# Norm factors and a bias row sent through memory, and gate sums scanned on VectorE, in place of fp32 products on TensorE

## What is computed

```python
def swiglu_ffn(x, g, w_gate, w_up, w_down):
    h = rms_norm_2(x, g)                       # x * rsqrt(mean(x*x) + eps) * g, a factor per token
    return (silu(h @ w_gate) * (h @ w_up)) @ w_down

# second block, forgetting attention: 8 heads, log_f is (256 tokens, 8 heads)
log_f = log_sigmoid(ff + b_forget)
cum = cumsum(log_f, axis=1).transpose(0, 2, 1)             # per head, along the tokens
logits = logits + cum[:, :, start:end, None] - cum[:, :, None, :end]

# second block, sparse attention: a bias per head and per bucket of the distance t - s (32 buckets)
bias = rel_bias[bucket]
```

## Time and profile before

| | us |
|---|---|
| median of three runs | 1117.91 (1117.83 to 1118.14) |
| the profiled execution, device time | 1117.82 |
| its span, first to last instruction of the program | 1116.0 |
| PE busy | 1110.3 (99%) |
| DVE busy | 786.0 (70%) |
| ACT busy | 621.3 (56%) |
| POOL busy | 57.7 (5%) |

### The profile page before, as it was taken

One profiled execution on the slowest core, in us unless ns is written; L12 is line 12 of the kernel. 1 busy time (PEld: TensorE's weight loads), 2 busy tenths in 40 slices (PEclk: granted clock), 3 DMA queues, 4 the chain that ended last, 5 costly groups with the idle time before them and its releaser, 6 DMA issues.

```text
span 1116.0 us, 14890 instructions
## 1 busy us (share of the span) xinstructions
PE 1110.3 (99%) x5854; PEld 944.4 (85%) x5854; DVE 786.0 (70%) x1112; ACT 621.3 (56%) x825; POOL 57.7 (5%) x105
## 2 busy tenths in 40 slices
PE   9999999999999999999999999999999999999998
PEld 8888888888888888888888888888888788888887
DVE  6777754766887677775477787557898686777752
ACT  6556542677566455564346556337787854656540
POOL 1000000100000000000000000021343000000000
PEclk9999999999999999999999999999999999999999
DMA  9765565644454656655565555557643455665550
GB/s 317 250 189 189 190 244 190 209 158 144 162 193 157 207 188 189 189 189 189 189 208 187 190 189 189 189 154 256 223 146 122 150 176 166 189 190 193 191 180 38
DMA packets 142581, 208.02 MB, mean 186 GB/s; under 512 B 9296, under 2 KB 100584, under 8 KB 142512
## 3 DMA queue, kind: packets, MB, share of 16 engines
q1 hardware_dynamic: 139408, 198.07, 54.1%
q0 software_dynamic: 3088, 9.00, 2.4%
q10 hardware_dynamic: 16, 0.00, 0.0%
HBM read 205.98 MB, written 2.65 MB: 187 GB/s over the span
## 4 chain that ended last, share of the span: by engine, by line
PE 96%; ACT 2%; DVE 1%; issue 1%; DMA 0%; SPq 0%; DVEq 0%
PE banks L1800 27%; PE banks L1686 16%; PE banks L1688 16%; PE banks L1687 16%; PE banks L1797 14%; PE banks L1758 1%; PE banks L2031 1%; PE banks L1708 1%; PE banks L1976 1%; ACT w_hi L751 0%; DMA raw<-in_ffn_w_gate 0%; PE banks L2061 0%; DVE w_lo L1138 0%; PE banks L2009 0%; PE banks L2058 0%
## 5 line engine op out<-in xcount | busy, mean ns | idle before, releaser
L1138 DVE TENSOR_TENSOR w_lo<-raw,w_hi 128x2048 fp32r<-128x2048 f32 x186 | 422.8, 2276 | 167.0 <-ACT w_hi L751 166.6
L751 ACT ACTIVATE w_hi<-raw 128x2048 fp32r<-128x2048 f32 x186 | 352.2, 1897 | 111.9 <-PE banks L1688 108.2
L1800 PE MATMUL banks<-xT,w_hi 128*128 128x512 f32 x1344 | 314.3, 390 | 0.0
L1800 PEld LDWEIGHTS banks<-xT,w_hi 128*128 128x128 f32 x1344 | 249.3, 188 | 49.8
L1797 PEld LDWEIGHTS banks<-xT,w_lo 128*128 128x128 f32 x1344 | 167.4, 191 | 4.1 <-DVE xg L1152 0.7
L1686 PE MATMUL banks<-w_hi,xT 128*128 128x512 f32 (+1 forms) x432 | 170.4, 394 | 0.0
L1797 PE MATMUL banks<-xT,w_lo 128*128 128x256 f32 x1344 | 169.8, 283 | 0.2
L1688 PE MATMUL banks<-w_hi,xT 128*128 128x512 f32 (+1 forms) x432 | 166.9, 386 | 0.0
L1687 PE MATMUL banks<-w_lo,xT 128*128 128x512 f32 (+1 forms) x432 | 166.7, 386 | 0.0
L1686 PE MATMUL banks<-w_hi,hT_hi 128*128 128x512 f32 x352 | 137.3, 390 | 0.0
L1688 PE MATMUL banks<-w_hi,hT_lo 128*128 128x512 f32 x352 | 137.0, 389 | 0.0
(11 more groups left out here) (315 smaller groups left out, 902.6 us busy)
## 6 DMA issues: line engine op xcount, KB each, us to landing
raw<-in_ffn_w_gate SPq DMA_DIRECT2D x88, 512.0 KB, 3.9
raw<-in_ffn_w_up SPq DMA_DIRECT2D x88, 512.0 KB, 4.9
raw<-in_ffn_w_down SPq DMA_DIRECT2D x88, 512.0 KB, 4.3
raw<-in_w_in SPq DMA_DIRECT2D x76, 512.0 KB, 4.5
raw<-in_w_out SPq DMA_DIRECT2D x16, 512.0 KB, 4.2
raw<-in_w_branch_moba SPq DMA_DIRECT2D x4, 512.0 KB, 4.2
raw<-in_w_branch_sb SPq DMA_DIRECT2D x4, 512.0 KB, 5.2
raw<-in_w_branch_a SPq DMA_DIRECT2D x4, 512.0 KB, 4.3
```

Source lines behind the costliest of these rows:

```text
L751: act.activation(w_hi[u % SLOTS][:, 0:n], raw[u % RAWS][:, 0:n], ACT.Copy).then_inc(hi_done, 1)
L1138: dve.tensor_tensor(w_lo[r][:, 0:n], raw[r][:, 0:n], w_hi[u % SLOTS][:, 0:n], ALU.subtract).then_inc(lo_done, 1)
L1800: m = pe.matmul(bank[b + s], mh, xT[:, k].rearrange("p a s -> p (a s)"), start=first, stop=k == KC - 1, skip_group_check=c == 0)
```

## The change

Three things are replaced, and the table of one-hot values is no longer sent to the chip.

Norm factors: in each of the four FFN phases POOL waits for the factors, writes them as a row to memory (`norm_rows`, 256 elements of 4 bytes), waits for that, and reads the row repeated on 128 partitions into `rstd_rows`, which now has a buffer of its own. DVE waits for this transfer ahead of its first `pair_scale`. The diagonal, the product and the copy are gone, and with them PE's waits for them.

Bias row: POOL reads the table transposed (8 by 32, elements of 4 bytes) and writes `lag_rows` by one copy for each range of distances that shares a bucket, 32 of them, in F0 right after the first gain transfer. The product, ACT's copy and the one-hot transfer are gone; the writing to memory and the spread there (L671, L673) follow right after, earlier than before.

Gate sums: the item CU is gone. POOL writes `log_f` transposed to memory by two transfers of 1024 elements of 4 bytes, waits for both, and reads it back as 8 rows of 256. In slot 14 DVE waits for that, sums along the rows by one scan, turns the sign and copies the first half. POOL's chain to the masks then starts from there.

```diff
-        out = [(6, "TR", ("iq", 0)), (7, "TR", ("iq", 1)), (9, "TR", ("ik", 0)), (12, "CU", ())]
+        out = [(6, "TR", ("iq", 0)), (7, "TR", ("iq", 1)), (9, "TR", ("ik", 0))]
...
+            rstd_rows = hid.enter_context(nc.sbuf_tensor("rstd_rows", [P, SEQ], F32))[:]
...
+        log_in = cum_last[0:NH, SC:SC + SEQ]
...
-        rstd_diag = gate[:, 0, 0:SEQ]
-        rstd_rows = gate[:, 1, DM:DM + SEQ]
-        onehot = gate[0:32, 1, 0:SC]
+        bias_cols = gate[0:NH, 1, 0:32]
...
+            def spread_rows(ph):
+                f, g = FFN_OF[ph], GAIN_OF[ph]
+                pool.wait_ge(rstd_done, g + 1)
+                pool.dma_start(norm_rows[f].rearrange("(t p) -> p t", p=P), rstd[:, 2 * g:2 * g + 2],
+                               allow_slow_non_contiguous=True).then_inc(rstd_out, 16)
+                pool.wait_ge(rstd_out, 16 * (f + 1))
+                pool.dma_start(rstd_rows, norm_rows[f].partition_broadcast(P)).then_inc(rows_in, 16)
...
-            pool.dma_start(onehot, a["onehot"]).then_inc(table_in, 16)
-            pool.dma_start(lgt[0:32, 0:NH], a["rel_bias_2"]).then_inc(table_in, 16)
+            pool.dma_start(bias_cols, a["rel_bias_2"].rearrange("b h -> h b"), allow_slow_non_contiguous=True)\
+                .then_inc(table_in, 16)
             pool.wait_ge(hi_done, 4)
             pool.dma_start(const[:, P:C_ONE], a["consts"][:, P:C_ONE]).then_inc(const_in, 16)
             pool.dma_start(tri_le, a["consts"][:, C_LE:C_GE]).then_inc(const_in, 16)
+            spread_rows("F0")
             for m in range(1, 7):
...
                 pool.dma_start(gain[m % 2][:], a[gains[m]].partition_broadcast(P)).then_inc(gain_in, 16)
+                if m == 4:
+                    spread_rows("F1")
+                    spread_rows("F2")
                 if m == 1:
+                    pool.wait_ge(table_in, 16)
+                    for k, (c0, c1) in lag_ranges():
+                        ins = pool.tensor_copy(lag_rows[:, c0:c1], bias_cols[:, k:k + 1].to_broadcast([NH, c1 - c0]))
+                    ins.then_inc(vrow_sb, 1)
                     pool.wait_ge(vrow_sb, 1)
...
-            cu = [it for it in ITEMS[1] if it.kind == "CU"][0]
-            pool.wait_ge(read_a, cu.read)
+            pool.wait_ge(rows_ready, 3)
+            for t in range(TT):
+                pool.dma_start(log_rows[:, t * P:(t + 1) * P].rearrange("h p -> p h"), lgf[:, NH * t:NH * t + NH],
+                               allow_slow_non_contiguous=True).then_inc(log_out, 16)
+            pool.wait_ge(log_out, 32)
+            pool.dma_start(log_in, log_rows).then_inc(log_row_in, 16)
+            pool.wait_ge(summed, 1)
             pool.dma_start(cum_rows, ncum).then_inc(cum_out, 16)
...
+            spread_rows("F3")
...
-                for tt in range(TT):
-                    dve.tensor_scalar(rstd_diag[:, tt * P:(tt + 1) * P], ident, rstd[:, 2 * g + tt:2 * g + tt + 1],
-                                      None, ALU.mult).then_inc(diag_done, 1)
...
-                    dve.wait_ge(rows_copied, FFN_OF[ph] + 1)
+                    dve.wait_ge(rows_in, 16 * (FFN_OF[ph] + 1))
...
+                def sum_log():
+                    dve.wait_ge(log_row_in, 16)
+                    link(dve.tensor_tensor_scan(ncum[:, P:SC], log_in, log_in, 0.0, ALU.add, ALU.min))
+                    link(dve.tensor_scalar(ncum[:, P:SC], ncum[:, P:SC], -1.0, None, ALU.mult))
+                    dve.tensor_copy(ncum[:, 0:P], ncum[:, P:SEQ]).then_inc(summed, 1)
...
+                        if slot == 14:
+                            sum_log()
...
-                if c == 2 and p == 1:
-                    pe.wait_ge(rows_copied, FFN_OF[ph] + 1)
...
-                pe.wait_ge(diag_done, 2 * FFN_OF[ph] + 2)
-                pe.matmul(bank[3][:, 0:SEQ], ones, rstd_diag, start=True, stop=True).then_inc(rows_mm, 1)
...
-                        pe.matmul(bank[1][0:NH, 0:SC], lgt[0:32, 0:NH], onehot, start=True, stop=True)\
-                            .then_inc(vrow_mm, 1)
...
-                    pe.matmul(S[0:NH, 0:P], lgf[:, 0:8], tri_le, start=True, stop=True)
-                    pe.matmul(S[0:NH, P:SEQ], lgf[:, 0:8], ones, start=True, stop=False)
-                    pe.matmul(S[0:NH, P:SEQ], lgf[:, 8:16], tri_le, start=False, stop=True).then_inc(scored, 1)
```

More of the change, by code:

```diff
@@ L150, in plan @@
             it.m_odd = kind in ("SM", "SB") and m % 2 == 1
-            it.reader = "a" if kind in ("IX", "CU") else "d"
+            it.reader = "a" if kind == "IX" else "d"
             reads[it.reader] += 1
@@ L349, in build @@
         hT_lo_done = sem("hT_lo_done")
-        diag_done = sem("diag_done")
-        rows_mm = sem("rows_mm")
-        rows_copied = sem("rows_copied")
+        rstd_out = sem("rstd_out")
+        rows_in = sem("rows_in")
         pair_done = sem("pair_done")
@@ L392, in build @@
         scaled_d = sem("scaled_d")
+        log_out = sem("log_out")
+        log_row_in = sem("log_row_in")
+        summed = sem("summed")
         cum_out = sem("cum_out")
@@ L405, in build @@
         lnf = sem("lnf")
-        vrow_mm = sem("vrow_mm")
         vrow_sb = sem("vrow_sb")
@@ L430, in build @@
         cum_rows = nc.dram_tensor("cum_rows", [NH, SC], F32).ap()
+        log_rows = nc.dram_tensor("log_rows", [NH, SEQ], F32).ap()
+        norm_rows = nc.dram_tensor("norm_rows", [4, SEQ], F32).ap()
         ffn_w = [("ffn1_w_gate", "ffn1_w_up", "ffn1_w_down"), ("ffn2_w_gate", "ffn2_w_up", "ffn2_w_down"),
@@ L805, in first_hidden_hi @@
                 act.activation(hT_hi[:, 0:2, :], bank[2].rearrange("p (k t) -> p k t", k=2), ACT.Copy).then_inc(hT_hi_done, 1)
-            def rstd_rows_in(ph):
-                act.wait_ge(rows_mm, FFN_OF[ph] + 1)
-                act.activation(rstd_rows, bank[3][:, 0:SEQ], ACT.Copy).then_inc(rows_copied, 1)
             def low(ph, c, p):
@@ L884, in ffn @@
                         split_hi(u)
-                    if ph == "F0" and s == NCH + 1:
-                        act.wait_ge(vrow_mm, 1)
-                        act.activation(lag_rows, bank[1][0:NH, 0:SC], ACT.Copy).then_inc(vrow_sb, 1)
                     if ph == "F0" and s == NCH + 2:
@@ L943, in gate_rows @@
                                        scale=r(tt)).then_inc(gated, 1)
[L945 to L948, removed]
                 def turn(it):
@@ L1065, in mixer @@
                     for it in ITEMS[b]:
-                        if slot - it.slot == 1 and it.kind == "CU":
-                            sum_rows(it)
                         if slot - it.slot == 1 and it.kind == "IX":
@@ L1288, in ffn @@
                     rms(GAIN_OF[ph])
-                spread_rstd(ph)
+                halve_rstd(ph)
                 if ph in FIRST_OF:
@@ L1821, in pair_chunk @@
                     pair_products(ph, c, 0, p, False)
-                if c == 1 and ph not in FIRST_OF:
-                    spread_rows(ph)
                 for p in range(2):
@@ L1827, in pair_chunk @@
                 if c == 1 and ph == "F0":
-                    spread_rows(ph)
+                    turn_hidden(ph)
                 pair_second(ph, c)
@@ L1917, in ffn @@
                     m.then_inc(unit_used, 1)
-                    if ph == "F0" and d == 1:
-                        pe.wait_ge(table_in, 32)
-                        pe.wait_ge(pair_summed, pairs_before(ph, NCH - 1) + 1)
-                        pe.matmul(bank[1][0:NH, 0:SC], lgt[0:32, 0:NH], onehot, start=True, stop=True)\
-                            .then_inc(vrow_mm, 1)
             def mixer(b):
@@ L1930, in mixer @@
                     pe.wait_ge(const_in, 32)
-                    pe.wait_ge(vrow_sb, 1)
                 def score_bank(it):
@@ L2118, in mixer @@
                             turn(it)
-                        if it.kind == "CU" and d == 0:
-                            sum_rows(it)
                         if it.kind in ("SM", "SB", "IX") and d == 0:
@@ L2172, in lag_buckets, with lag_ranges @@
     return np.where(lags < exact, lags, np.minimum(large, n_buckets - 1))
+def lag_ranges():
+    import numpy as np
+    bucket = lag_buckets(32, 128, np.maximum(SEQ - 1 - np.arange(SC), 0))
+    ends = [0] + [c for c in range(1, SC) if bucket[c] != bucket[c - 1]] + [SC]
+    return [(int(bucket[c0]), (c0, c1)) for c0, c1 in zip(ends, ends[1:])]
 def constants():
@@ L2185, in constants @@
     c[:, C_LE:C_LE + P] = p <= f
-    bucket = lag_buckets(32, 128, np.maximum(SEQ - 1 - np.arange(SC), 0))
-    onehot = (np.arange(32)[:, None] == bucket[None, :]).astype(np.float32)
-    return c, onehot
+    return c
 def kernel(**inputs):
@@ L2198 @@
     arrays, aps = {}, {}
-    consts, onehot = constants()
-    shape_only = {"consts": consts, "onehot": onehot}
+    shape_only = {"consts": constants()}
     for name, v in {**inputs, **shape_only}.items():
```

14 lines of the change are left out of this document (1 added, 13 removed).

## The result

The changed kernel takes **1152.88 us** (median of four runs, 1151.43 to 1154.95) against 1117.88 us of the kernel before on the same chip: 1.0314 times as long, 95% interval 1.0302 to 1.0326. The prediction of 1116.8 us, and its range up to 1120.2, were wrong, and so was the sign. The profiled execution took 1152.41 us with a span of 1150.6, against a span of 1116.0 before.

A forecast was written before the change was run, and what follows sets the result against it. PE, busy 99% of the span, was taken as the bound. Spreads -1.70, one-hot product -0.95, DVE late at slot 19 +0.73, masks +0.93 gave -1.0 us: 1116.8 from 1117.82, range for 8 in 10 1114.2 to 1120.2.

The forecast's parts named there:

- That is 6.3 us by the nearest rows, between 5.6 and 8.6: FFN phases: time for the factor rows to be written to memory and read back on 128 partitions; lateness costed at zero.
- I take 8 us: M1: write and read-back of the log rows, bounds 6.5 and 11.5 us, against 10.2 us of room before DVE's slot 14.
- B: M1: log rows late, DVE stands in slot 14, PE at its transposes; 1118.1 to 1125.7 us; chance 17%.
- C: F1 and F3: factor rows late by more than 3.3 us each; one us past that in each gives 1118.8; chance 4%.
- The room in F1: F1: 6.7 us from factors ready to DVE's first scale, and 3.3 us more lateness covered until PE asks for the split.
- each us beyond that is a us of the whole: M1: log rows landing later than 10.2 us after `log_f` lengthen the whole time by one us per us.
- the most that this change can give: PE: all removed products together (four spreads, one-hot product, gate sums) save 3.6 us.
- its 0.95: PE: removing the bias row's one-hot product saves 0.95 us, its replacement on POOL costing zero.
- The sums' 0.95: M1: removing the gate sums' products takes 0.95 us off PE, not kept, as DVE makes PE go on 0.73 later.
- The four spreads' 1.7: FFN phases: removing PE's four factor spreads, 0.42 us each, saves 1.7 us.
- Rival A: M1: DVE has more room than forecast, so the whole 3.6 us come through, 1114.2 us; chance 18%.
- the 0.93 of the sum: M1: POOL's masks start 3.6 us later and run beside DVE's norms, slowing four instructions: 0.93 us added.

The follow-up runs named there:

- Probes: The kernel before plus rows of unused POOL transfers in F0, three kernels; in the first, 256 values took 11.1 us as 4-byte neighbours, 5.9 as 8-byte pairs.
- the mended kernel: The whole change, but factors written in pairs of 8 bytes and sums at the end of slot 17: 1114.91 us, ratio 0.9975 to the kernel before.
- the packed rows alone: The kernel before with only the factor rows through memory, written in pairs of 8 bytes and read by DVE with a stride: 1118.23 us, ratio 1.0001.

## Why the prediction was wrong

**The step that failed: the transfers.** "That is 6.3 us by the nearest rows, between 5.6 and 8.6" for the factor rows: measured 17.8 us in F1 (write to landing 9.0, 0.3, read 8.5) and 15.6 to 20.8 in the four phases. "I take 8 us" with 11.5 at most for the log rows: measured 17.4 us. Both upper bounds were wrong at the write. For the log rows its price came from transfers that *read* memory, the narrow weight load (512 pieces of 32 bytes in 1.9 us) and toep (pieces of 1 KB); for the factor rows from the 1.7 us of a write with pieces of 1536 bytes, made 2.4 by "pieces of its own". Measured were 9.7 and 10.2. No row showed a write in 4-byte pieces, and the prediction said so ("No row here has 4-byte writes to memory"), and then gave the matter to B alone, at 17%, while C got 4%. The two rest on the same unknown, and the chances should have been tied: a write of 9.7 us alone nearly fills the 10 us of room that C has. The read of the factor rows was over its bound of 5.9 us too (up to 8.5, median 7.4); behind packed writes it took 5.5. Probes put about 6 us on a read behind a 4-byte write, so what made it 8.5 in F1 is open.

**What was said about the rest of the chain held.** The room in F1 was put at 6.7 us to the scale and 3.3 more until PE asks for the split, 10.0 in all; a chain of 17.8 us is 7.8 too long, and PE stood for 8.42. That "each us beyond that is a us of the whole" held for the sums, nearly: with them alone DVE waited 7.23 us, PE 8.0, and the time rose by 8.8. F2, with the most room, had a gap of 1.0 only.

**Not in the sum at all: the clock.** B and C were priced at one us per us. The slower matmuls behind the gaps added 7.9 us to 29.7, about a quarter more.

**Products.** 3.6 us was "the most that this change can give"; PE's busy time fell by 3.0 between the kernel before and the mended one. The bias row gave its 0.95 (1.0 measured) at no cost elsewhere, as predicted. The sums' 0.95 was said not to be kept, as DVE sets when PE goes on at the transposes of slot 19. With the sums moved to slot 17 PE starts these at 804.18 in place of 804.93, so 0.75 was kept there, and the new wait for the masks among the attention heads took a part back; the last sentence of the prediction had named such a gap. The time fell by 0.4, which its interval doesn't tell from none. The four spreads' 1.7 came as about 1.2 in the mended kernel (the 1.6 us without the masks' 0.4), and not at all with the packed rows alone, where F3's wait took 1.0 and the rest is open. Rival A's 1114.2, in which everything comes through, is nearly what the mended kernel does.

**Masks.** They did come later, and they met the norms: in the kernel after they run from 821.6 to 827.4, and beside them DVE's L1383 takes 0.58 us (0.24 before), L1392 0.65 and L1393 0.66 (0.64 and 0.67 before), while L1391 stays at 0.18 and the products at L1397 at 1.29. That is 0.3 us more than before, not the 0.93 of the sum. With the transfers from SBUF to SBUF the products beside the masks took 2.32 in place of 1.29, and PE stood 0.4 at slot 19 behind them, so the term is real there.

## What to carry to other kernels

Don't turn a column into a row by a memory write of single elements side by side: keep what a partition holds together in one piece, and let the consumer's access pattern do the rest; if it must be turned, turn it on the way into SBUF (11.5 us here against 17.4). A chain that can't be made short can be made harmless by the place where the in-order engine comes to it, and that cost one moved line here; the wait that may come up further down (here 0.8 us for the masks) has to be looked for. And when a price stands in no row of the trace, all steps that rest on it fall together: measure it by a transfer that nobody uses before building on it.

## What the runs showed of the hardware

**4-byte writes side by side are late after the data has moved.** In F1 of the kernel after, the window from 395 to 397 us holds the write's 32 packets (queue q0), and the one from 397 to 402.9 holds none of q0, though the transfer lands only at 402.9 (the queues in the two windows: packets, MB, share of 16 engines):

```profile
q1 hardware_dynamic: 29, 0.03, 12.1%
q0 software_dynamic: 32, 0.00, 2.6%
```
```profile
DMA packets 303, 0.31 MB, mean 52 GB/s; under 512 B 2, under 2 KB 303, under 8 KB 303
...
q1 hardware_dynamic: 303, 0.31, 24.5%
```

The last q0 packet starts at 395.5, 1.6 us after the issue; the landing comes 7.4 us later, and the engines are busy for a quarter of that time only, with 52 GB/s. With pairs of 8 bytes the last packet of the same write is at 390.5 and the landing at 394.08, 3.6 us later. With 4-byte pieces it matters whether they touch: 7.6 to 11.1 us side by side over the three probes, 3.7 to 4.6 when 64 bytes apart, 2.7 to 4.0 when 512 apart; the last two overlap, so no run tells them apart. No run looks into the memory, and why pieces that touch land late stays open.

The Trainium skill (DMA: Bandwidth & Descriptors, "Anatomy of one DMA") has a fixed cost of about 2.0 us that is mostly the write's receipt and calls it constant. The trace agrees for the 12 KB write before (1.7 us) and for the 32-byte pieces in M1 (1.7), less for the 12 KB write in the kernel after (3.4), and not for 4-byte neighbours: there the time behind the last packet, where the receipt lies, is 7.4 us. The limit of 512 bytes that the Trainium skill gives (DMA: Bandwidth & Descriptors, "Specifications") doesn't sort these writes either: pieces of 32 bytes and pieces of 4 bytes both lie below it, and took 1.7 and 9.8 us in the same place of M1. In F0, beside the weight loads, the pieces of 32 bytes took 3.5 to 5.4 us.
